# Low weight parts of three stages made by accumulating DMAs, and modulation units reordered in attention

## The reference, cut to what matters

```python
shift, scale, gate = split(silu(c) @ mod_w[i] + mod_b[i], 3)
h = rms_norm(x, norm_g[i]) * (1 + scale) + shift
# layer 0, LRU: u, g = split(h @ w_in); conv of u, two gates per direction, linear scans; y = (scans) * silu(g)
# layer 1, attention: q, k, v, g = split(h @ w_in), 16 heads; softmax(q1 k1) - lam * softmax(q2 k2); y = norm(o) * silu(g)
# layers 2 and 3, SGU and grouped attention: u, v, z, q, k, v, zb = split(h @ w_in); y = cat(sgu * silu(z), attn * silu(zb))
x = x + gate * (y @ w_out)
```

## Time and profile before

| quantity | value |
|---|---|
| median of 3 runs | 3095.57 us (3093.31 to 3095.76) |
| the profiled execution's own time | 3095.1 us |
| its span, first to last instruction | 3093.4 us |
| mean granted TensorE clock | 0.937 of 2.4 GHz |
| TensorE busy, VectorE busy, ScalarE busy, GpSimd busy | 87%, 70%, 39%, 7% of the span |
| bytes moved by DMA | 488.82 MB, 158 GB/s over the span |

### The profile page before, as it was taken

The page is one execution under the profiler, slowest core; times in us unless marked ns, Lnnn a source line. Parts: engine busy times, 40 slices in busy tenths (PEclk is TensorE's granted clock), DMA queues, the critical chain, the costliest instruction groups (busy, mean ns, idle before and its releaser), DMA issues.

```text
span 3093.4 us, 41399 instructions
## 1 busy us (share of the span) xinstructions
PE 2694.4 (87%) x13746; PEld 2201.3 (71%) x13746; DVE 2150.8 (70%) x3280; ACT 1203.8 (39%) x1839; POOL 218.3 (7%) x241
## 2 busy tenths in 40 slices
PE   3799989899777787887887799999999899899989
PEld 1376767578566666666666687878788688798879
DVE  2488888999857787878878658888455422654654
ACT  2254545622333333333323443232344422553653
POOL 0100000033200000000000140000000022200000
PEclk9699989899889898898998899999999999799999
DMA  6854544557444444444444354776222132353324
GB/s 256 335 181 147 186 159 168 181 187 226 144 163 162 137 163 136 150 148 144 155 155 142 123 180 163 245 236 226 96 80 70 44 111 103 116 184 123 133 92 170
DMA packets 134268, 488.82 MB, mean 158 GB/s; under 512 B 14896, under 2 KB 21296, under 8 KB 129584
## 3 DMA queue, kind: packets, MB, share of 16 engines
q1 hardware_dynamic: 124960, 439.58, 42.3%
q0 software_dynamic: 9232, 48.24, 4.1%
HBM read 485.66 MB, written 2.10 MB: 158 GB/s over the span
## 4 chain that ended last, share of the span: by engine, by line
PE 48%; DVE 26%; issue 11%; DMA 8%; ACT 6%; DVEq 1%; ACTq 0%; SPq 0%; POOL 0%; POOLq 0%
PE psum L273 13%; PE psum L274 13%; PE psum L275 13%; DVE work L323 5%; DMA mw<-in_mod_units 4%; DVE w_lo L244 4%; DVE mw L325 3%; DMA y<-in_mod_weights 2%; DMA y<-in_x_t 1%; PE psum L694 1%; DVE y L1082 1%; DVE y L323 1%; ACT w_hi L236 1%; DVE h_lo L453 1%; PE psum L1427 1%
## 5 line engine op out<-in xcount | busy, mean ns | idle before, releaser
L273 PE MATMUL psum<-h_hi,w_hi 128*128 128x512 f32 (+1 forms) x3840 | 1383.4, 360 | 46.1 <-DVE h_lo L453 39.6
L274 PE MATMUL psum<-h_lo,w_hi 128*128 128x512 f32 (+1 forms) x3840 | 1341.1, 349 | 0.0
L275 PE MATMUL psum<-h_hi,w_lo 128*128 128x512 f32 (+1 forms) x3840 | 1339.8, 349 | 0.0
L273 PEld LDWEIGHTS psum<-h_hi,w_hi 128*128 128x128 f32 x3840 | 741.5, 193 | 168.1 <-DVE h_lo L453 38.5
L244 DVE TENSOR_TENSOR w_lo<-raw,w_hi 128x1024 fp32r<-128x1024 f32 x496 | 589.0, 1229 | 364.8 <-ACT w_hi L236 360.9
L274 PEld LDWEIGHTS psum<-h_lo,w_hi 128*128 128x128 f32 x3840 | 742.0, 193 | 99.8 <-issue 13.7
L275 PEld LDWEIGHTS psum<-h_hi,w_lo 128*128 128x128 f32 x3840 | 739.6, 193 | 91.0
L236 ACT ACTIVATE w_hi<-raw 128x1024 fp32r<-128x1024 f32 x496 | 496.7, 1052 | 385.6 <-PE psum L275 370.0
L325 DVE SCALAR_TENSOR_TENSOR mw<-mw,cb 128x1024 f32<-128x1024 f32 x256 | 318.3, 1243 | 0.0
L323 DVE SCALAR_TENSOR_TENSOR work<-mw,cb 128x1024 bf16<-128x1024 f32 x208 | 267.8, 1287 | 0.2 <-DMA mw<-in_mod_units 0.2
L332 DVE SCALAR_TENSOR_TENSOR mw<-mw,cb 128x1024 f32<-128x1024 f32 x64 | 78.0, 1224 | 61.8 <-DMA mw<-in_mod_units 61.6
(11 more groups left out here) (252 smaller groups left out, 2676.2 us busy)
## 6 DMA issues: line engine op xcount, KB each, us to landing
raw<-in_weights SPq DMA_DIRECT2D x496, 512.0 KB, 4.4
mw<-in_mod_units SPq DMA_DIRECT2D x320, 512.0 KB, 4.2
cb<-in_mod_weights POOLq DMA_DIRECT2D x16, 1024.0 KB, 7.7
y<-in_mod_weights POOLq DMA_DIRECT2D x16, 1024.0 KB, 9.1
cb<-in_cond_rows SPq DMA_DIRECT2D x4, 1024.0 KB, 6.9
work<-in_gate_w POOLq DMA_DIRECT2D x16, 256.0 KB, 4.1
work<-in_x_t POOLq DMA_DIRECT2D x16, 256.0 KB, 3.5
xl<-in_x_t SPq DMA_DIRECT2D x1, 2048.0 KB, 39.9
```

The costliest lines, as they stand in the source:

```text
L273: pe.matmul(dst, hi, h_hi[:, k, 0:n], start=(k == 0), stop=False)
L274: pe.matmul(dst, hi, h_lo[:, k, 0:n], start=False, stop=False)
L275: mm = pe.matmul(dst, lo, h_hi[:, k, 0:n], start=False, stop=(k == KT - 1))
```

## The change

For 120 strips (2 to 33, 50 to 113 and 132 to 155, the ranges `DMA_LO`) ScalarE writes the rounded half twice, first negated into `w_lo` and then into `w_hi`, and a DMA that GpSimd issues adds the raw half to `w_lo` in SBUF. The other strips (`DVE_LO`) are split by VectorE as before. TensorE and SyncE wait for these DMAs' semaphores (`wait_lo`) in place of VectorE's. In attention the four units of a head, which stood behind each `w_lo`, now stand behind the norm of k (unit 0), behind the norm of q (unit 1) and behind the rotation of q (units 2 and 3). ScalarE's `cb_tanh` of head 1 moves to the end of that head's list. SyncE's list is written to match, and the loops of GpSimd in LRU, attention and SGU are written out.

```diff
+DMA_LO = [(S_LRU + 2, S_LRU_OUT + 2, 2), (S_ATT + 2, S_ATT_OUT + 2, 18), (S_NET2 + 2, S_NET2 + L2_KV + 2, 34)]
+DVE_LO = [(0, 2, 0), (34, 50, 32), (114, 130, 96), (154, N_STRIPS, 120)]
+        def wait_lo(eng, st, half):
+            if st.dma:
+                eng.wait_ge(S["split_hi"], 2 * st.s + half + 1)
+                eng.wait_ge(lo_in[2 * st.par + half], LO0 + 16 * (st.pair - st.dma[0] // 2 + 1))
+            else:
+                eng.wait_ge(S["split_lo"], 2 * (st.s - st.dve[0]) + half + 1)
+        def load_next(sp, base, c, j=0, per=2):
+            st = Strip(base, c, j, per)
+            load_strip(sp, st.pair + 1, st.par, st)
+        def split_neg(act, pair, par):
+            s = 2 * pair + par
             for half in range(2):
...
+                act.activation(w_lo[:, par, half, :], raw[:, 2 * par + half, :], ACT.Copy, scale=-1.0).then_inc(S["split_neg"], 1)
+                act.activation(w_hi[:, par, half, :], raw[:, 2 * par + half, :], ACT.Copy).then_inc(S["split_hi"], 1)
+        def add_raw(pool, base, c, j=0, per=2):
...
+            for half in range(2):
+                pool.wait_ge(S["split_neg"], 2 * (st.s + 2 - off) + half + 1)
+                pool.dma_start(w_lo[:, st.par, half, :], raw[:, 2 * st.par + half, :], accum_op=ALU.add).then_inc(lo_in[2 * st.par + half], 16)
...
                 for c in range(2):
-                    next_strip(split_lo_pool, pool, Strip(S_LRU, 2 * par + c, j, 4))
+                    add_raw(pool, S_LRU, 2 * par + c, j, 4)
...
-                next_strip(split_hi, act, su)
+                next_strip(split_neg, act, su)
...
-                next_strip(split_lo_dve, dve, su)
                 unit(dve, 5 * j + 2 * par, 0, 4 * j + 2 * par)
...
                 if here:
-                    next_strip(split_lo_dve, dve, att_strip(j, par, 0))
-                    units(j, par, 0)
...
-                    next_strip(split_lo_dve, dve, att_strip(j, par, 1))
-                    units(j, par, 1)
...
-                    next_strip(split_lo_dve, dve, att_strip(j, par, 2))
-                    units(j, par, 2)
+                    units(j, par, 0)
...
-                    next_strip(split_lo_dve, dve, att_strip(j, par, 3))
-                    units(j, par, 3)
+                    units(j, par, 1)
...
                     dve.tensor_tensor(qr, qr, rtmp, ALU.add).then_inc(A["qr"], 1)
+                    units(j, par, 2)
+                    units(j, par, 3)
...
+            def head(j, par, order=((0,), (), (1, 2), (3,))):
+                for c in range(4):
+                    for n in order[c]:
+                        unit_load(sp, U_ATT + 4 * (2 * j + par) + n)
+                    load_next(sp, S_ATT + 2, 4 * par + c, j, 8)
```

More of the change, by code:

```diff
@@ L236, in split_hi, with split_lo @@
                 act.activation(w_hi[:, par, half, :], raw[:, 2 * par + half, :], ACT.Copy).then_inc(S["split_hi"], 1)
-        def split_lo(eng, pair, par, halves=(0, 1)):
+        def split_lo(dve, pair, par, halves=(0, 1)):
             s = 2 * pair + par
[L240 to L256, removed]
+            for half in halves:
+                dve.wait_ge(S["split_hi"], 2 * s + half + 1)
+                if half == 0:
+                    ge(dve, S["strip_done"], s - 1)
+                dve.tensor_tensor(w_lo[:, par, half, :], raw[:, 2 * par + half, :],
+                                  w_hi[:, par, half, :].bitcast(F32), ALU.subtract).then_inc(S["split_lo"], 1)
         def next_strip(split, eng, st):
@@ L515, in out_first @@
                 if kk == 0:
-                    pe.wait_ge(split_lo_done[half], out_strip[l] + 2)
+                    for c in range(2):
+                        wait_lo(pe, Strip(out_strip[l], c), half)
                 pe.wait_ge(S["y_ready"], KT * l + k + 1)
@@ L672, in lru_pool @@
                 gates(b, b)
-            take_over(pool, S_LRU + 2)
             block(0, 0, first=True)
             block(0, 1)
-            with pool.Fori(1, BLOCKS // 2 - 1) as j:
+            for j in range(1, BLOCKS // 2):
                 for par in range(2):
-                    block(j, par)
-            for par in range(2):
-                block(BLOCKS // 2 - 1, par, last=par == 1)
+                    block(j, par, last=2 * j + par == BLOCKS - 1)
         def lru_pe(pe):
@@ L1156, in sgu_pool @@
             group(0, 1)
-            with pool.Fori(1, GROUPS // 2 - 1) as j:
+            for j in range(1, GROUPS // 2 - 1):
                 for par in range(2):
@@ L1799, in _ @@
             sp.wait_ge(S["cb_ready"], 8)
-            with sp.Fori(4, 2 * HEADS1) as j:
+            with sp.Fori(1, HEADS1 // 2) as j:
+                for par in range(2):
+                    head(j, par)
+            with sp.Fori(0, KT // 2) as j:
                 for c in range(2):
-                    unit_load(sp, U_ATT + 2 * j + c)
-                    load_strip(sp, S_ATT // 2 + 2 + j, c)
-            with sp.Fori(S_ATT_OUT // 2 + 2, S_NET2 // 2 + 2) as pair:
-                for par in range(2):
-                    load_strip(sp, pair, par)
+                    load_next(sp, S_ATT_OUT + 2, c, j)
             sp.wait_ge(A["qr"], HEADS1)
```

118 lines of the change are left out of this document (60 added, 58 removed).

## The result

The changed kernel took 3120.95, 3127.38 and 3130.91 us, a median of 3127.38; the ratio to before is 1.0102, 95% interval 1.0075 to 1.0129. It is 1.0% slower where 2973 us and faster was forecast. The range, 2870 to 3140, holds it. (One correction to the text above: the third range of `DMA_LO` is strips 130 to 153.)

What follows compares the result with a forecast made beforehand. No stage was full of TensorE work at full clock; attention lost most, to VectorE's order of work. Attention -132, LRU -27 and SGU +37 sum to -122 us, from 3095.1 to 2973 us; range 2870 to 3140.

Steps and rivals of the forecast that it cites:

- The price of an add: All three stages: an accumulating DMA of 512 KB takes two passes, 2.8 us of the 16 DMA engines.
- the waits at L918 and L933: Attention: TensorE's waits for VectorE there, 40.6 and 25.0 us before the change, would go.
- they finish some 4 us after the next k strip, hidden by ScalarE's splits: Attention: units 2 and 3, now ending a head, finish 4 us after the next k strip, covered by ScalarE's splits.
- rival 3: Attention and LRU: VectorE's freed time is not TensorE's, maxima come late; head 52 us, kernel 3057 us; chance 0.08.
- 10 us of VectorE work leave each head: Attention: the argument given against rival 3, that VectorE loses 10 us of work a head.
- a head above 50 at a share under 0.8: Attention: the sign, with the share that of the DMA engines, that would prove the latency or the order wrong.
- The sum's 45: Attention: TensorE's head, 42.5 us at full clock plus 2 of idle, called 45; 47.5 with DMA interference.
- I take 40.5: SGU: a group takes 40.5 us, from 38.9 us of DMA demand and SyncE's delayed units; loss 37 us.
- so nothing: SGU: GpSimd's table load, which waits for y with adds behind it, costs nothing.
- the next split at 12: SGU: y comes 10 us into a group and the next split at 12 us.
- Rival 2: All stages: adds are dear and DMA becomes the bound, deciding from 3.5 us an add; 3245 us at 4.2; chance 0.25.
- That gives 27.7 ... 55 us: LRU: a block's chain takes 27.7 us, two blocks 55 us with TensorE's waits; gain 27 us.

Runs made afterwards that it cites:

- e5: Changed kernel with adds in attention alone, a head's fourth unit and `unit_sum` moved behind the next head's maxima; 2964.8 us, ratio 0.9573.
- e13: Changed kernel with the SGU's raw loads issued by GpSimd behind the adds instead of by SyncE; 3128.49 us.
- e16: Changed kernel with GpSimd's SGU table load behind the group's three adds instead of behind the first; 3109.03 us.
- e8: Changed kernel with unit loads of 64 KB in place of 512 KB, the rest of each unit left out; 2940.6 us.
- e17: Changed kernel with e9's orders, VectorE's SGU list turned over (y first, norm of v before units 2 to 4) and e16's table load; 3011.55 us.
- e9: e5 plus adds in the LRU, where a block's second unit moves behind the next block's convolution; 2946.7 us, ratio 0.9515.
- e12: e9 with the LRU's low parts made by VectorE again, so that stage has only the new order; 2952.63 us.
- e15: e13 with unit loads cut to 64 KB as in e8; 2915.54 us.
- e10: Changed kernel with SGU units 1 and 2 each loaded ahead of the raw load before them in SyncE's list; 3135.71 us.

## Why the prediction was wrong

**What was right.** The price of an add (2.71 us for 2.8), its latency (7.1 for 7), ScalarE's negating copies (1.052), the DMA share, the waits at L918 and L933. The rule of the Trainium skill that a reduction in the DMA engines runs at half the rate of a copy ("Collectives: The Full Stack", section "The bandwidth ceiling: the fold count and why AG ≠ RS ≠ AR") was nearly borne out: 2.71 against 1.53 us, a factor of 1.77. That the range holds the result is luck: its upper end stood for adds of 3.7 us, and no add cost that. The misses of the three stages, 52, 27 and 40 us, are 119 of the 148 between the forecast sum and the profiled execution. The other 29 lie outside the landmarks, 17 of them between attention and the SGU and 6 behind the SGU, and the prediction had no term for them.

**Attention, -80 instead of -132.** The step that failed: "they finish some 4 us after the next k strip, hidden by ScalarE's splits". They finish 8.3 us after it, and the splits (to 1352.4) end 6 us before the exponentials can start. A unit half took 4.4 us to land in the sum. In that stage it took 6.1, and unit 2's second half, among two adds and two raw loads, 8.5. That is rival 3, maxima late by units: 52 us was its head, 51.0 was measured. It had a chance of 0.08, because "10 us of VectorE work leave each head"; but that work left other places in VectorE's list than the one ahead of the maxima, where one unit and a `w_lo` gave way to the last two units of the head. e5 settles it: one unit fewer ahead of the maxima, and the head is at 45.5 us with every add still there. The sign given for this case, a head above 50 at a share under 0.8, was too narrow: late loads and a share of 0.91 came together. The late start also cost clock: after its 7.3 us of waiting TensorE had a granted clock of 0.50 from 1363 to 1366 us. The sum's 45 took full clock; over 1000 to 1500 us it was 0.91, in e5 0.98.

**SGU, +77 instead of +37.** The step that failed is "I take 40.5", volume, 38.9 us of the engines, and 1.6 for order. The volume was somewhat larger: a share of 0.90 of 46.6 us is 42 us of the engines, as plain transfers beside adds cost 1.5 us (41.95 MB at 52.0% over 1884 to 2115 us) where 1.39 was taken. That is 3 of the 6 us by which a group was missed. For the rest the engines idle, and the sum had no term for it: the two unit halves, each landing and then used by VectorE five times a group. By the estimate under e13, before's 4.1 us of landing gives 32 us, under the group's 35.4, so the turn did not show, though the chain had unit loads at its head. Where the list does not hold the loads back the landing beside adds is 6.5 us in e16 and 6.9 in e13, and the estimate 44.0 and 46.0, for groups of 44.4 and 46.6. In the changed kernel itself a unit half lands after 4.5 us (median), but SyncE's list holds the loads back, 71 of 220 us, for adds. List and turn are about equally long, so taking away one of them shortens nothing (e13) or every second group (e8). Two smaller steps failed too: "so nothing" for the table load (1.3 us a group by e16, nothing by e17, though the changed kernel's timeline has an add 6.7 us late), and "the next split at 12", when y has come late by the units itself. Rival 2's +67 to +97 for this stage was right in size, not in cause: its adds were to cost 3.5 us and more.

**LRU, 0 instead of -27.** "That gives 27.7 ... 55 us" took the convolution to follow y by the second unit's 4.9 us only. In the changed kernel it also had waits for unit loads (L357, 47.8 us in the stage where the earlier trace rows has 19.3) and TensorE's gates behind a wait at a granted clock of 0.50, where the sum took full clock: three products take 2.92 us where one at full clock has a median of 0.59. (The kernel before had that as well: eight behind a wait took 6.72 us for 4.7.)

```profile
402.22 2.92 PE L715 MATMUL psum<-work 128*128 128x512 f32 x3 [5.85 <-DVE work L799]
```

With small loads a pair takes 54.7 us (e8), and with the unit behind the convolution 21 of the 27 us come (e9), 10 of them without any add (e12). How much each of the two waits costs is not parted.

One error lies behind all three: the landing time of plain loads was carried over from the kernel before (4.4 us) into a schedule whose queues would be twice as busy, and only their volume was summed. In attention and LRU it did harm because units stood ahead of what others wait for; in e5 loads land later still, and the head is short.

## What to carry to other kernels

When work moves to the DMA engines, price two things: the engines' time, and the longer landing of every other load; then multiply the second through each chain of load, use and next load over few buffers, because such a chain can become the bound before the share reaches 1 (here at 0.90). Freed time on an engine helps the path only where it stands ahead of what others wait for: list that engine's order again and move what nobody awaits (here the units) behind it. Apply such a change stage by stage: the same edit was worth -80, 0 and +77 us in three stages, and the stages with slack (attention, LRU) without the third give 2946.7 us, 4.9% under before. The late order in attention without adds was not tried, so how much of e5's gain needs the adds stays open; in the LRU about half of the gain came without them (e12).

## What was not expected of the hardware

A load is slowed by what other queues carry: in the SGU unit loads of 64 KB landed after 2.8 us in e8 (1720 to 1960 us), but after 4.1 in e15, where GpSimd's queue carried the raw loads beside the adds and the share was 0.82 for 0.72. The DMA engines can run at a share of 0.99 for 500 us (e5, 275 GB/s) with TensorE at 94% busy and a clock of 0.98. And where the share rose from 0.45 to 0.91 (1000 to 1500 us) the landing of a 512 KB load rose from 4.0 to 4.2 us to 6.1 to 6.4 (medians); adds landed after 6.7 us there and after 10.6 in e10's SGU (1889 to 2123 us), the longest median of these runs.
